# The first two weight chunks of a prompt projection, fetched before the stage that multiplies them

## What is computed

```python
h = rms(x, norm1_g) * (1.0 + sc1) + sh1
z = h @ w_in                 # (1024, 1024) @ (1024, IN_W)
q_nsa, kv_new, win_new, nsa_gl, q_dif, merge_l = split(z)
# merge_l (2048 columns) gates the two attention branches, through a sigmoid
# the other 1944 columns are queries, keys, values and small gates
```

## Time and profile before

| | us |
|---|---|
| median of 3 runs | 2302.58 |
| lowest, highest | 2302.22, 2305.25 |
| the profiled execution, whole | 2303.02 |
| its span, first to last instruction | 2301.3 |
| mean granted TensorE clock, share of full speed | 0.939 |

### The profile page before, as it was taken

One profiled execution on the slowest core, in us unless ns is written; L12 is line 12 of the kernel. 1 busy time (PEld: TensorE's weight loads), 2 busy tenths in 40 slices (PEclk: granted clock), 3 DMA queues, 4 the chain that ended last, 5 costly groups with the idle time before them and its releaser, 6 DMA issues. The chain is left out here.

```text
span 2301.3 us, 34001 instructions
## 1 busy us (share of the span) xinstructions
PE 2081.8 (90%) x12158; PEld 1787.5 (78%) x12158; DVE 1166.7 (51%) x2320; ACT 620.0 (27%) x1181; POOL 140.8 (6%) x187
## 2 busy tenths in 40 slices
PE   6979999969996999985887969699999999999996
PEld 1339889849995989983667957499899899998994
DVE  0433333332235666664887744455645646545547
ACT  2113334411223665651773012221111111111100
POOL 0030000010300000000102000000000000000003
PEclk9989999989996999895999989899999999999997
DMA  9765445212101000000002441131110111111104
GB/s 313 253 197 174 140 144 166 71 46 69 47 2 59 1 0 0 0 0 0 1 0 92 126 167 47 57 91 28 55 55 27 55 50 32 55 31 51 36 0 157
DMA packets 132688, 166.64 MB, mean 72 GB/s; under 512 B 15891, under 2 KB 98675, under 8 KB 132548
## 3 DMA queue, kind: packets, MB, share of 16 engines
q1 hardware_dynamic: 117790, 134.75, 18.5%
q0 software_dynamic: 5008, 17.71, 2.4%
q10 hardware_dynamic: 9808, 13.11, 1.7%
HBM read 144.87 MB, written 22.77 MB: 73 GB/s over the span
## 5 line engine op out<-in xcount | busy, mean ns | idle before, releaser
L1634 DVE TENSOR_TENSOR late_x<-late_x,ffn_po 128x512 f32<-128x512 f32 (+1 forms) x396 | 257.1, 684 | 2.0
L1619 DVE TENSOR_TENSOR ffn_av<-ffn_pv,ffn_sg 128x344 f32<-128x344 f32 x66 | 34.1, 516 | 339.2 <-PE ffn_pv L1567 339.2
L1534 ACT ACTIVATE ffn_sg<-ffn_pg 128x344 f32<-128x344 f32 x66 | 30.2, 458 | 586.6 <-PE ffn_pg L1567 586.6
L1567 PE MATMUL ffn_pg<-late_words_hi,ffn_uhi 128*128 128x344 f32 x528 | 170.1, 322 | 14.9 <-DVE ffn_ulo L1601 14.9
L1567 PE MATMUL ffn_pg<-late_words_lo,ffn_uhi 128*128 128x344 f32 x528 | 169.7, 321 | 0.0
L1567 PE MATMUL ffn_pg<-late_words_hi,ffn_ulo 128*128 128x344 f32 x528 | 169.6, 321 | 0.0
L1567 PE MATMUL ffn_pv<-late_words_hi,ffn_uhi 128*128 128x344 f32 x528 | 168.6, 319 | 0.0
L1567 PE MATMUL ffn_pv<-late_words_lo,ffn_uhi 128*128 128x344 f32 x528 | 168.5, 319 | 0.0
L1567 PE MATMUL ffn_pv<-late_words_hi,ffn_ulo 128*128 128x344 f32 x528 | 168.3, 319 | 0.0
L1583 PE MATMUL ffn_po<-ffn_ohi,ffn_a_hi 128*128 128x512 f32 (+1 forms) x396 | 157.5, 398 | 7.2 <-DVE late_x L1634 7.2
L1583 PE MATMUL ffn_po<-ffn_olo,ffn_a_hi 128*128 128x512 f32 (+1 forms) x396 | 157.7, 398 | 0.0
(11 more groups left out here) (451 smaller groups left out, 4546.7 us busy)
## 6 DMA issues: line engine op xcount, KB each, us to landing
mod_wr<-in_w_ada SPq DMA_DIRECT2D x12, 2048.0 KB, 8.9
ffn_raw_u<-in_w_ffn_in SPq DMA_DIRECT2D x44, 512.0 KB, 5.7
dec_kin<-in_cache_kv SPq DMA_DIRECT2D x64, 256.0 KB, 3.5
ffn_raw_o<-in_w_ffn_out SPq DMA_DIRECT2D x22, 512.0 KB, 3.8
gate_d<-dec_gate ACTq DMA_DIRECT2D x48, 172.0 KB, 2.2
late_x<-gate_d SPq DMA_DIRECT2D x8, 1032.0 KB, 5.4
dec_raw<-in_w_in POOLq DMA_DIRECT2D x16, 512.0 KB, 5.5
dec_vin<-in_cache_kv SPq DMA_DIRECT2D x64, 128.0 KB, 2.1
```

What stands on the lines that cost most here:

```text
L1534: act.activation(sg[(j + c) % 2][:], pg[(j + c) % 2][:, 0:TCH], ACT.Silu).then_inc(silu_done, 1)
L1567: mm = pe.matmul(bank[b][:, 0:TCH], w[j][:, v * KD + k, :], h[:, k, tok], start=(k == 0 and q == 0), stop=(k == KD - 1 and q == 2))
L1619: dve.tensor_tensor(av[b][:], pv[b][:, 0:TCH], sg[b][:], ALU.mult).then_inc(a_done, 1)
L1634: dve.tensor_tensor(part, part, po[(j * NO + u) % 4][0:r, :], ALU.add).then_inc(o_read, 1)
```

## The change

The first projection chunk gets tiles of its own that live from the gate and decode stage on: zraw, zhi and zlo, of 324 columns by 8 blocks on each partition. They take the place of kin. The key pages are given the same addresses (a scope is opened and closed for them, and a pad keeps the total the same), and so the new tiles may be written only when kin has been read. For this SyncE waits in the gate and decode stage for the last pair's counts: kt_full, sq_done, ks_done and sv_done. It then fetches chunk one into zraw, VectorE splits it at half step 90 into zhi and zlo, and when this is done (z_lo) SyncE fetches chunk two into the same zraw (z_next). The read-back od moves from kin to the space of the value pages.

In the projection, zraw, zhi and zlo are used as raw, whi[0] and wlo[0]. VectorE's split(0) and the first two fetches are gone, TensorE's first unit waits for no weights, and the counts of w_in, w_hi and w_lo are lower by the steps taken away.

```diff
@@ project_token_major
-        raw = s.sb("raw", [P, KD, ZCH])
-        whi = [s.sb(f"whi{i}", [P, KD, ZCH], F32R) for i in range(2)]
-        wlo = [s.sb(f"wlo{i}", [P, KD, ZCH], F32R) for i in range(2)]
+        raw, hi0, lo0 = g.zraw[:], g.zhi[:], g.zlo[:]
+        whi = [hi0, s.sb("whi1", [P, KD, ZCH], F32R)[:]]
+        wlo = [lo0, s.sb("wlo1", [P, KD, ZCH], F32R)[:]]
...
-                    if n:
-                        sp.wait_ge(raw_free, n)
-                    sp.dma_start(raw[:], w[:, :, c * ZCH:(c + 1) * ZCH]).then_inc(w_in, 16)
+                    if n >= 2:
+                        sp.wait_ge(raw_free, n - 1)
+                        sp.dma_start(raw, w[:, :, c * ZCH:(c + 1) * ZCH]).then_inc(w_in, 16)
...
                     j = n % 2
-                    dve.wait_ge(w_in, n * 16 + 16)
                     if n >= 2:
+                        dve.wait_ge(w_in, n * 16 - 16)
                         dve.wait_ge(acc_full, (n - 1) * TT)
-                    dve.tensor_copy(whi[j][:], raw[:]).then_inc(w_hi, 1)
-                    dve.wait_ge(w_hi, n + 1)
-                    dve.tensor_tensor(wlo[j][:], raw[:], f32(whi[j][:]), ALU.subtract).then_inc(w_lo, 1)
-                    dve.wait_ge(w_lo, n + 1)
+                    else:
+                        dve.wait_ge(g.z_next, 16)
+                    dve.tensor_copy(whi[j], raw).then_inc(w_hi, 1)
+                    dve.wait_ge(w_hi, n)
+                    dve.tensor_tensor(wlo[j], raw, f32(whi[j]), ALU.subtract).then_inc(w_lo, 1)
+                    dve.wait_ge(w_lo, n)
...
-                split(0)
                 split(1)
...
-                    if t == 0:
-                        pe.wait_ge(w_lo, n + 1)
+                    if t == 0 and n:
+                        pe.wait_ge(w_lo, n)
@@ gates_and_decode
-        kin = s.sb("kin", [P, 2, NPAGE, KW])
+        kin = g.kin
...
-        od = kin[0:NDEC].rearrange("p x t c -> p (x t c)")[:, 0:NH * 5 * HD].rearrange("p (h c) -> p h c", h=NH)
+        od = early[:, 0:NH * 5 * HD].rearrange("p (h c) -> p h c", h=NH)
+        zraw, zhi, zlo = g.zraw[:], g.zhi[:], g.zlo[:]
...
+                sp.wait_ge(kt_full, (NP - 1) * NY + 8)
+                sp.wait_ge(sq_done, NP * 5)
+                sp.wait_ge(ks_done, NP)
+                sp.wait_ge(sv_done, NP)
+                sp.dma_start(zraw, w[:, :, Z_ORDER[0] * ZCH:(Z_ORDER[0] + 1) * ZCH]).then_inc(z_in, 16)
+                sp.wait_ge(z_lo, 1)
+                sp.dma_start(zraw, w[:, :, Z_ORDER[1] * ZCH:(Z_ORDER[1] + 1) * ZCH]).then_inc(g.z_next, 16)
                 sp.wait_ge(o_out, NP * 16)
                 sp.dma_start(od, io["dec_d"].rearrange("(b r) c -> b r c", r=8)).then_inc(od_in, 16)
...
+                    if H == HALVES - 6:
+                        dve.wait_ge(z_in, 16)
+                        dve.tensor_copy(zhi, zraw).then_inc(z_hi, 1)
+                        dve.wait_ge(z_hi, 1)
+                        dve.tensor_tensor(zlo, zraw, f32(zhi), ALU.subtract).then_inc(z_lo, 1)
                 outputs(NP - 1)
@@ trunk_step
+            with Scope(nc, "kin") as kin:
+                g.kin = kin.sb("kin", [P, 2, NPAGE, 512])
+            g.zraw = h.sb("zraw", [P, KD, ZCH])
+            g.zhi, g.zlo = (h.sb(x, [P, KD, ZCH], F32R) for x in ("zhi", "zlo"))
+            h.sb("pad", [P, 2 * NPAGE * 512 - 3 * KD * ZCH])
+            g.z_next = h.sem("z_next")
             gates_and_decode(nc, io, g)
```

More of the change, by code:

```diff
@@ L298, in _ @@
                     dve.tensor_copy(g.zd[:, c:c + ZC], pm[n % 3][0:NDEC, 0:ZC]).then_inc(z_sb, 1)
+Z_ORDER = [4, 5, 0, 1, 2, 3]
 def project_token_major(nc, io, g, a):
     NM6 = ZW // ZCH
-    ORDER = [4, 5, 0, 1, 2, 3]
+    ORDER = Z_ORDER
     g.tsel = a.sb("tsel", [P, SEQ])
@@ L1779, in gates_and_decode @@
         o_out, od_in = s.pool_sem("o_out"), s.sem("od_in")
+        z_in, z_hi, z_lo = s.sem("z_in"), s.sem("z_hi"), s.sem("z_lo")
         w = io["w_in"][0].rearrange("(k p) n -> p k n", p=P)
```

## The result

| | median us | lowest, highest | ratio to before | 95% interval |
|---|---|---|---|---|
| before, 4 runs | 2303.66 | 2302.22, 2305.25 | | |
| after, 4 runs | 2291.34 | 2290.24, 2292.69 | 0.9947 | 0.9929 to 0.9964 |

The kernel is 12.3 us faster.

The account below looks back on a forecast made before the run. TensorE's work plus the stretches in which it stands still were taken to bound the kernel. From the earlier median of 2302.58 us, 11.71 us removed and 0.4 us added for the clock gave 2291.3 us, range 2289.6 to 2294.4.

Parts of the forecast that it names:

- What is removed: Between decode and projection: chunk one's fetch and split leave the path, so the first projection matmul starts 11.71 us earlier.
- The clock: At the projection's start: TensorE's clock still falls in the gap, and a slow restart of 5.0 us adds 0.4 us.
- What is added in decode: In decode: the added SyncE waits and fetches, VectorE's split and the moved read-back cost 0.
- Left in the projection: In the projection: chunk two is split with 25 us spare and no later chunk is late.
- later than 505: Sign of being wrong: the first projection matmul comes after 505 us with nothing named as its releaser.
- late start: Rival at the barrier into the projection: TensorE starts up to 4.6 us late, 2291.3 to 2295.9 us; chance 0.08.
- later than 487: Sign of being wrong: VectorE's outputs at the end of decode come after 487 us.
- held tail: Rival in decode's tail: the split or transfers delay the barrier, up to 6.2 us, giving 2297.5 us; chance 0.05.
- before 680: Sign of being right: the last projection matmul comes before 680 us, where TensorE was busy up to 688 at least.
- within 0.5: Sign of being right: the first projection matmul comes within 0.5 us of VectorE's last decode operation.
- slower end: Rival in decode: a late chunk-one transfer holds VectorE's last outputs and the kernel ends slower, 2313.9 us; chance 0.02.
- nothing: Rival at the first projection matmul: something other than fetch and split holds it, so no change, 2302.6 us; chance 0.02.

Follow-up runs that it names:

- e2: Changed kernel, but chunk one is only fetched in decode and split in the projection, and chunk two is fetched in the projection: 2296.17 us, ratio 0.9971.
- e9: Changed kernel with one more wait, so the fetch of chunk one is sent only when decode's last values are through: 2303.62 us, ratio 1.0008.
- e1: The changed kernel run again without any edit: 2291.55 us, ratio 0.9951 to the kernel before.
- e5: Changed kernel with 58 throwaway matmuls appended to TensorE's decode program to keep it busy through the gap: 2289.32 us, ratio 0.9939.
- e4: Changed kernel keeping only the new tiles, pad, scope and read-back place, with both chunks fetched and split in the projection: 2302.67 us, ratio 0.9997.
- e6: Changed kernel with the fetch of chunk two moved behind the last outputs, ahead of the decode result's write and read-back: 2295.04 us, ratio 0.9965.
- e7: Changed kernel with TensorE computing the first two token tiles of chunk one at the end of decode: 2285.16 us, ratio 0.9926.
- e3: Changed kernel with chunk two fetched only in the projection, chunk one still fetched and split in decode: 2291.43 us, ratio 0.9949.
- e10: Changed kernel with chunk two fetched in the projection and chunk one's split moved behind the last outputs, into the read-back wait: 2291.91 us, ratio 0.9955.

## Why the prediction was right

*What is removed.* 11.71 us were predicted, and the first matmul did start 11.68 us earlier: 508.38 - 489.39 = 18.99 us behind the last value products against 516.06 - 485.39 = 30.67. Two small errors cancel in it. The crossing of the barrier takes 0.53 us and not 0.33, in the change, e2 and e9 alike. And the tail was 17.40 us long (490.45 to 507.85) instead of 17.56, as the read-back took 4.85 and not 5.02 us.

*The clock.* It fell although the gap was halved and rose 4.8 us after the restart (5.2 in e1), where 5.0 was assumed. That 5.0 was the middle of 4.0, 4.5 and 6.0 at three other places, so its closeness is in part luck. The windows in which it changes, beside the earlier trace rows:

```profile
500.00:504.00 4.00, 0.00 (x0) 0.00 (x0) 3.79 (x8) 0.00 (x0) 0.00 (x0) 0.86 0.01 3
513.00:513.50 0.50, 0.50 (x5) 0.50 (x4) 0.00 (x0) 0.00 (x0) 0.50 (x1) 0.86 0.00 0
```

The border lost 11.68 - 11.38 = 0.30 us of the gain by it; 0.4 were predicted. In e1 the first matmul starts as early (18.98 us behind the value products) and the border gives 11.17, so there it is 0.5. e5 shows the whole restart at 2.1 us; 2.2 were predicted.

*What is added in decode.* Cost 0 held for all of it. SyncE sent the fetches at 447.73 and 474.98, which is 443.8 and 471.8 moved by the 4 us of the slow stretch, less 0.7 for the shorter subtraction. VectorE was free 15.50 us before its outputs (14.7 predicted; the subtraction took 2.86 us without GpSimd beside it, not 3.58). e4 shows the layout free. e6 and e9 show what it costs to leave that cover: 3.5 us if one transfer meets the round trip, all of the gain if the fetch waits for the last values.

*Left in the projection.* TensorE has no wait in it. Windows, beside the earlier trace rows:

```profile
516.00:680.00 164.00, 164.00 (x1111) 164.00 (x1110) 48.28 (x72) 35.91 (x85) 23.43 (x26) 1.00 0.09 30
```

From the eighth result of the projection to the last takes 142.0 us in the change and all eleven experiments, and 142.2 before. So what was gained at the border was kept.

*The signs.* Read by absolute times, three signs went against the prediction: the first matmul at 508.38 ("later than 505" stood for a late start), VectorE's outputs at 490.45 ("later than 487" stood for a held tail), and the last projection matmul ending at 681.2 instead of before 680. All three are the slow stretch near 350. In e1, the same kernel without it, they are 502.54, 484.62 and 675.5. The signs that count from a neighbouring event held, but for the first matmul at 0.53 us behind VectorE's last decode operation where "within 0.5" was asked.

*The rivals.* The late start did not happen (0.53 us). The held tail, the slower end and "nothing" did not either, but the first two are real mechanisms, as e6 and e9 show. The held tail cost 3.5 us, where up to 6.2 were given. For the slower end the prediction had break-even where VectorE passes its wait 48.8 us behind 443.8, that is at 492.6; e9 passes it at 494.05, 1.4 us later, with its last values at 485.44 as before's at 485.39. Its first projection matmul starts 1.1 us later behind them than before (31.75 against 30.67), and its border is 0.67 us longer.

*The sum.* 2291.3 against 2291.34 and 2291.55. It is closer than it deserved: 16 runs of the kernel before on one chip went from 2300.82 to 2306.73, and the slow stretch near 350 alone moved a profile by 4.6 us. What the mechanism can be held to is the border: 11.4 and 11.2 us against 11.3 predicted.

## What to carry to other kernels

A gap between two stages has parts with different owners: read which of them your change can remove, and what the other then is. Here the fetch and the split were 11.2 us of 21.9, and the other half was TensorE waiting for a chain of small operations. Once the first chunk was ready early, that half could be filled with the next stage's own matmuls for another 11.8 us, of which about 2 are the slow restart that goes with the gap.

Work moved ahead of a barrier is free only if each queue it is put in has time there, and only as long as the event that releases it is early. Judge a change of 0.5% on a stretch close around it, not on absolute times of two profiles.

## What was not expected of the hardware

The clock of TensorE falls at different distances behind its last matmul: 2.0 us before (494.18 to about 496.2), 4.7 us after (497.85 + 0.32 to about 502.9), and in e7, after a pause of 3.49 us, only when TensorE had been working again for over 1 us (restart at 502.88, mean of 0.97 for 494 to 505). In one place of decode it is low for a short or for a long time in executions of the same code, while TensorE is busy: 0.92 against 0.69 over 22 us, with the work behind it some 4.6 us later. Why it falls there was not tried.

VectorE's subtraction of 128 x 2592 takes 2.86 us alone and 3.58 us beside GpSimd's first operations, in the four profiles where the two meet (before, e3, e4, e10), and GpSimd's cast of 640 elements a partition takes 2.48 us beside it and 0.72 alone. Which of the two is held up differs: in e2 the second chunk's subtraction (516.83) still takes 2.86 us, and GpSimd's cast of 256 elements beside it takes 2.82 us instead of 0.40. The cast of 640 elements, before:

```profile
514.10 2.48 POOL L349 CAST at_twin<-z_iot 128x640 f32<-128x640 int32 x1
```

After:

```profile
517.06 0.72 POOL L352 CAST at_twin<-z_iot 128x640 f32<-128x640 int32 x1
```
